# Two transformer blocks on one core: the relative-bias table made by one 12-row matmul and a replicating store

## What is computed

```python
h = rms_norm(x, norm1_g)
proj = h @ w_in                                    # [256, 3072]: q_d, k_d, v_d, q_m, k_m, v_m, 512 columns each
q = rms_norm(q, q_g); k = rms_norm(k, k_g)         # over each head's 64 columns, for both kinds of attention
dist = qpos[:, None] - kpos[None, :]               # 256 x 256
bias = bias_table[t5_bucket(dist)]                 # bias_table is [32, 12]: 32 buckets, 12 heads
logits = where(dist >= 0, q @ k.T * scale + bias, -1e30)
```

## Time and profile before

| | before |
|---|---|
| median of 3 runs | 1170.93 us (1169.04 to 1173.18) |
| span of the profiled execution (the page has no other time for it) | 1172.5 us |
| TensorE busy (matmuls) | 94% |
| VectorE, ScalarE, GpSimd busy | 49%, 35%, 4% |
| DMA | 239.54 MB, 204 GB/s over the span |

### The profile page before, as it was taken

How to read it: one execution, slowest core, us unless ns; L and a number is a source line. 1 busy time by engine, 2 the same in 40 slices (tenths; PEclk the granted TensorE clock), 3 DMA queues, 4 the chain that set the end, 5 groups by cost and what they waited for, 6 DMA issues and landing times.

```text
span 1172.5 us, 15803 instructions
## 1 busy us (share of the span) xinstructions
PE 1103.3 (94%) x6625; PEld 885.3 (76%) x6625; DVE 574.5 (49%) x724; ACT 415.6 (35%) x518; POOL 41.3 (4%) x55
## 2 busy tenths in 40 slices
PE   6998899999999999999999999977899999999996
PEld 5866688454444448999999998856688889999995
DVE  4546836222222226444444548478765655444443
ACT  3424513111111114434433444364344334433431
POOL 1202000000000000000000000010000000000000
PEclk8979798999999999999999999877899999999999
DMA  8548029879999985555555354431055544555540
GB/s 237 191 148 292 1 108 374 331 321 390 418 407 416 415 308 170 183 183 185 172 186 184 132 188 153 144 108 36 1 198 182 196 161 160 182 179 179 179 144 36
DMA packets 101489, 239.54 MB, mean 204 GB/s; under 512 B 10966, under 2 KB 56098, under 8 KB 86082
## 3 DMA queue, kind: packets, MB, share of 16 engines
q1 hardware_dynamic: 99170, 229.05, 54.5%
q0 software_dynamic: 2272, 9.83, 2.5%
HBM read 235.45 MB, written 3.41 MB: 204 GB/s over the span
## 4 chain that ended last, share of the span: by engine, by line
PE 82%; DVE 9%; ACT 3%; issue 2%; DMA 1%; POOL 1%; SPq 1%; POOLq 0%; ACTq 0%; DVEq 0%
PE banks L910 18%; PE banks L912 17%; PE banks L911 17%; PE banks L1114 10%; PE banks L1129 5%; PE banks L1104 3%; PE banks L1095 3%; PE banks L917 2%; PE banks L984 1%; DVE weights_lo L1463 1%; PE banks L995 1%; PE banks L1229 1%; DMA bias_rows<-stage 1%; POOL head_stats L501 1%; ACT weights_hi L608 1%
## 5 line engine op out<-in xcount | busy, mean ns | idle before, releaser
L1463 DVE TENSOR_TENSOR weights_lo<-raw_weights,weights_hi 128x2048 fp32r<-128x2048 f32 x116 | 265.5, 2291 | 264.8 <-ACT weights_hi L608 264.8
L608 ACT ACTIVATE weights_hi<-raw_weights 128x2048 fp32r<-128x2048 f32 x116 | 221.9, 1914 | 317.2 <-PE banks L912 311.6
L910 PE MATMUL banks<-weights_hi,normed_T_hi 128*128 128x256 f32 (+1 forms) x976 | 307.6, 315 | 1.1 <-DVE normed_T_lo L1480 0.6
L912 PE MATMUL banks<-weights_hi,normed_T_lo 128*128 128x256 f32 (+1 forms) x976 | 304.8, 312 | 0.0
L911 PE MATMUL banks<-weights_lo,normed_T_hi 128*128 128x256 f32 (+1 forms) x976 | 304.8, 312 | 0.0
L910 PEld LDWEIGHTS banks<-weights_hi,normed_T_hi 128*128 128x128 f32 x976 | 187.3, 192 | 13.8 <-issue 2.0
L911 PEld LDWEIGHTS banks<-weights_lo,normed_T_hi 128*128 128x128 f32 x976 | 187.2, 192 | 10.9
L912 PEld LDWEIGHTS banks<-weights_hi,normed_T_lo 128*128 128x128 f32 x976 | 186.9, 191 | 10.4
L1114 PE MATMUL banks<-expert_weights,stage 128*64 128x512 f32 x256 | 113.2, 595 | 0.0
L910 PE MATMUL banks<-weights_hi,ffn_hidden_T_hi 128*128 128x512 f32 x176 | 68.9, 392 | 3.0 <-DVE ffn_hidden_T_lo L1775 3.0
L911 PE MATMUL banks<-weights_lo,ffn_hidden_T_hi 128*128 128x512 f32 x176 | 68.7, 390 | 0.0
(11 more groups left out here) (305 smaller groups left out, 1597.1 us busy)
## 6 DMA issues: line engine op xcount, KB each, us to landing
raw_weights<-in_w_in SPq DMA_DIRECT2D x38, 1024.0 KB, 5.1
raw_weights<-in_ffn_w_gate SPq DMA_DIRECT2D x22, 1024.0 KB, 5.6
raw_weights<-in_ffn_w_up SPq DMA_DIRECT2D x22, 1024.0 KB, 5.6
raw_weights<-in_ffn_w_down SPq DMA_DIRECT2D x22, 1024.0 KB, 4.7
expert_weights<-in_w_gate SPq DMA_DIRECT2D x16, 1024.0 KB, 7.1
expert_weights<-in_w_up SPq DMA_DIRECT2D x16, 1024.0 KB, 9.2
expert_weights<-in_w_down SPq DMA_DIRECT2D x16, 1024.0 KB, 9.5
stage<-in_w_down SPq DMA_DIRECT2D x9, 1024.0 KB, 11.2
```

The lines of the kernel that those rows point to most:

```text
L608: ins = eng.activation(w_hi[:, slot, :], raw, ACT.Copy)
L910: eng.matmul(dst, x[0], w[0], start=first_one, stop=False)
L912: return eng.matmul(dst, x[1], w[0], start=False, stop=last_one)
L1463: ins = eng.tensor_tensor(w_lo[:, slot, :], raw, w_hi[:, slot, :], ALU.subtract)
```

## The change

The 12 matmuls, the spread table and the 12 copies become one matmul with 12 output rows, one copy of 12 x 384, and a store whose source repeats each of the 12 rows 128 times, so that DRAM receives the same 2.36 MB as before. That matmul and the transpose of the small vectors move between the first and the second half product of group 0; VectorE's part of both moves behind `feed(0)`. The store and load on GpSimd stand, in its order, ahead of the roots of all four q and k groups instead of between the second and the third. In each q or k group, VectorE makes the sums of squares of both tiles before it splits the next piece, and scales afterwards; each tile has a scratch place of its own.

```diff
-        bias_stage = LP[:, 0:N_BIAS * DIST_COLS].rearrange("p (h m) -> p h m", h=N_BIAS)
-        relb = LP[0:BUCKETS + 1, BS:BS + N_BIAS * P].rearrange("p (h q) -> p h q", h=N_BIAS)
+        bias_stage = LP[0:N_BIAS, 0:DIST_COLS]
+        onehot = LP[0:BUCKETS + 1, DIST_COLS:2 * DIST_COLS]
...
@@ gpsimd
-            for _ in range(2 * TILES):
-                root(hs[:, 0, 1, 0:8])
-            eng.wait_ge(bias_copied, N_BIAS)
-            eng.dma_start(bias_rows.rearrange("h p m -> p h m"), bias_stage).then_inc(bias_stored, 16)
+            eng.wait_ge(bias_copied, 1)
+            eng.dma_start(bias_rows, bias_stage.unsqueeze(1).broadcast_to([N_BIAS, P, DIST_COLS])).then_inc(bias_stored, 16)
             eng.wait_ge(bias_stored, 16)
...
             eng.dma_start(bias, skewed).then_inc(bias_loaded, 16)
             eng.wait_ge(normed, TILES * (N1 + 1))
             load_gain("norm2_g")
-            for _ in range(2 * TILES):
-                root(hs[:, 0, 1, 0:8])
+            for _ in range(4):
+                for t in range(TILES):
+                    root(hs[:, t, 1, 0:8])
@@ tensor
-            eng.wait_ge(vec_loaded, 16 * N_VEC)
-            eng.transpose(PS[:, 3, 0:V_ROWS], vec_rows[:, :], ident[0:V_ROWS, 0:V_ROWS]).then_inc(vec_T, 1)
             stay_warm(14, 2)
+            def small_tables():
+                eng.wait_ge(vec_loaded, 16 * N_VEC)
+                eng.transpose(PS[:, 3, 0:V_ROWS], vec_rows[:, :], ident[0:V_ROWS, 0:V_ROWS]).then_inc(vec_T, 1)
+                eng.wait_ge(rel_loaded, 32)
+                eng.matmul(PS[0:N_BIAS, 2, 0:DIST_COLS], relx[:, :], onehot[:, :], start=True, stop=True).then_inc(bias_ps, 1)
...
                 if c == 1:
                     eng.wait_ge(vec_ready, 1)
+                    eng.wait_ge(bias_copied, 1)
...
-                    if kh == 0 and c == 3:
-                        eng.wait_ge(rel_wide, 1)
-                        for h in range(N_BIAS):
-                            if h >= 2:
-                                eng.wait_ge(bias_copied, h - 1)
-                            eng.matmul(PS[:, 6 + h % 2, 0:DIST_COLS], relb[:, h, :], onehot[:, :], start=True, stop=True
-                                       ).then_inc(bias_ps, 1)
+                    if kh == 0 and c == 0:
+                        small_tables()
...
-            eng.wait_ge(bias_copied, N_BIAS)
@@ vector
             t8_split(T_N1, hT)
+            feed(0)
             eng.wait_ge(vec_T, 1)
...
-            feed(0)
-            eng.wait_ge(rel_loaded, 32)
-            eng.tensor_copy(relb[:, :, :], wide(relx[:, :], P)).then_inc(rel_wide, 1)
+            eng.wait_ge(bias_ps, 1)
+            eng.tensor_copy(bias_stage, PS[0:N_BIAS, 2, 0:DIST_COLS]).then_inc(bias_copied, 1)
...
+            def head_squares_of(c):
+                if c in (2, 5):
+                    return
+                for t in range(TILES):
+                    n = n_qk[0] + t
+                    eng.wait_ge(proj_sq, n + 1)
+                    eng.tensor_reduce(hs[:, t, 0, 0:8], tok[:, t, HALF:].rearrange("p (h d) -> p h d", d=HEAD),
+                                      AX_X, ALU.add).then_inc(proj_sq_read, 1)
+                    eng.wait_ge(proj_sq_read, n + 1)
+                    roots[0] += 1
+                    eng.tensor_scalar(hs[:, t, 1, 0:8], hs[:, t, 0, 0:8], 1.0 / HEAD, EPS, ALU.mult, ALU.add).then_inc(root_in, 1)
...
@@ vector, take_projection
-                    eng.wait_ge(proj_sq, n + 1)
-                    eng.tensor_reduce(hs[:, 0, 0, 0:8], tok[:, t, HALF:].rearrange("p (h d) -> p h d", d=HEAD),
-                                      AX_X, ALU.add).then_inc(proj_sq_read, 1)
-                    eng.wait_ge(proj_sq_read, n + 1)
-                    rsqrt(hs[:, 0, 1, 0:8], hs[:, 0, 0, 0:8], HEAD)
+                    eng.wait_ge(root_out, roots[0] - 1 + t)
...
             for c in range(6):
+                if c:
+                    head_squares_of(c - 1)
                 feed(2 * c)
                 if c:
                     take_projection(c - 1)
-                if c == 3:
-                    for h in range(N_BIAS):
-                        eng.wait_ge(bias_ps, h + 1)
-                        eng.tensor_copy(bias_stage[:, h, :], PS[:, 6 + h % 2, 0:DIST_COLS]).then_inc(bias_copied, 1)
```

More of the change, by code:

```diff
@@ L169, in two_blocks @@
         bias = view(6144, N_BIAS, SEQ)
-        bias_stage = LP[:, 0:N_BIAS * DIST_COLS].rearrange("p (h m) -> p h m", h=N_BIAS)
-        BS = N_BIAS * DIST_COLS
-        relb = LP[0:BUCKETS + 1, BS:BS + N_BIAS * P].rearrange("p (h q) -> p h q", h=N_BIAS)
-        onehot = LP[0:BUCKETS + 1, BS + N_BIAS * P:BS + N_BIAS * P + DIST_COLS]
-        lam_rows = LP[:, BS + N_BIAS * P + DIST_COLS:BS + N_BIAS * P + DIST_COLS + 4 * HEAD].rearrange("p (n d) -> p n d", n=4)
+        bias_stage = LP[0:N_BIAS, 0:DIST_COLS]
+        onehot = LP[0:BUCKETS + 1, DIST_COLS:2 * DIST_COLS]
+        lam_rows = LP[:, 2 * DIST_COLS:2 * DIST_COLS + 4 * HEAD].rearrange("p (n d) -> p n d", n=4)
         xgT = LP[:, 0:KT * RING * SLOTS].rearrange("p (k s) -> p k s", k=KT)
@@ L240, in two_blocks @@
         consts, root_in, root_out = sem("consts"), sem("root_in"), sem("root_out")
-        vec_T, vec_ready, rel_wide = sem("vec_T"), sem("vec_ready"), sem("rel_wide")
+        vec_T, vec_ready = sem("vec_T"), sem("vec_ready")
         bias_ps, bias_copied = sem("bias_ps"), sem("bias_copied")
@@ L1537, in take_projection @@
                     eng.tensor_tensor(tok[:, t, 0:HALF].rearrange("p (h d) -> p h d", d=HEAD),
-                                      bank.rearrange("p (h d) -> p h d", d=HEAD), wide(hs[:, 0, 1, 0:8], HEAD),
+                                      bank.rearrange("p (h d) -> p h d", d=HEAD), wide(hs[:, t, 1, 0:8], HEAD),
                                       ALU.mult).then_inc(proj_used, 1)
```

## The result

The changed kernel takes 1179.15 us (median of 9 runs, 1177.35 to 1181.44) against 1173.23 us of the kernel before (9 runs, 1169.04 to 1177.16): ratio 1.0052, 95% interval 1.0039 to 1.0066. It is 0.5% slower. The forecast was no change at 1171 with a range of 1151 to 1181; the time lies in the range, and the case that came is the third one, the slow store, to which I had given 0.30. The profiled span is 1177.4 us against 1172.5.

A forecast was written before the change was run, and what follows sets the result against it. TensorE was taken as the bound, its idle stretches, bias matmuls and low clock the time to win. Gains of 23.0 us, less the store's delay and 1.5 for the clock, gave 0.1: 1171 us at the median, range 1151 to 1181.

The forecast's parts named there:

- the slow store: Rival at GpSimd's wait ahead of the roots: shows slower from T = 34.6; at T = 39, net -7.9; chance 0.30.
- T: Time of GpSimd's bias store from 12 partitions, taken as 31 us, the middle by ratio of 12.9 and 74.
- net gain = 31.1 - T: Whole change: gains of 23.0 us, less the store's delay T - 9.6, less 1.5 for the clock.
- Start: Idle products right after the token transposes: first half product at 17.2 instead of 24.22, gain 7.0 us.
- Small tables: One vector transpose and one bias matmul between the first and second half product: cost 1.2 us.
- Bias matmuls and clock: TensorE's 12 bias matmuls from 65.17 go, 13.65 us, and the low clock after them, 1.3 us.
- VectorE order: Sums ahead of the split cover the roots: gain 0.8 after group 0, 1.2 after group 3, at most 0.2 after group 4.
- the 23.0: Sum of gains in us before the store's delay: 7.0 - 1.2 + 13.65 + 1.3 + 0.8 + 1.2 + 0.2.
- After the landing: GpSimd's load, gain load and roots, then scaling: TensorE's transposes end 6.6 us after the store lands.
- Clock after the hole: TensorE restarts at half clock after standing idle for the store: loss 1.5 us, between 0 and 2.6.
- Weights beside the store: About 1.3 weight pieces pass on the DMA queues beside the store; costed at nothing, up to 4 us if wrong.
- the fast store: Rival: source width does not matter, only engines; T 15.9, net 15.2 us; most of the 0.32 for faster.

The follow-up runs named there:

- changed_weights_early: The changed kernel, with SP issuing weight pieces 3 to 5 ahead of the router's and the gates' small loads; 1177.05 us, ratio 1.0026 to the kernel before.
- rows12_apart: The changed kernel, but the matmul gives 96 rows and the store reads 12 of them, 8 partitions apart, each 128 times; 1164.12 us, single run.
- rows24: The changed kernel, but the store reads 24 neighbouring rows, each 64 times; 1164.45 us, single run.
- rows96: The changed kernel, but the matmul gives 96 rows and the store reads all, each 16 times; 1160.76 us, ratio 0.9887 to the kernel before.
- tables_first: The changed kernel with the early start undone: small vectors and bias matmul ahead of idle products and first half product; 1179.38 us, ratio 1.0054.
- matmul_only: The kernel before with one 96-row bias matmul after group 3's first half product, its 96-row store at the old place; 1166.76 us, ratio 0.9935.
- order_only: The kernel before with only VectorE's new order, both tiles' sums ahead of the split; 1171.21 us, ratio 0.9980.
- rows96_roots_first: The changed kernel with 96 source rows and the four roots of groups 0 and 1 ahead of GpSimd's wait; 1151.30 us, ratio 0.9812.
- best_again: The kernel of rows96_roots_first measured a second time, unchanged; 1154.52 us, ratio 0.9829.
- roots_first: The changed kernel, but GpSimd serves the four roots of groups 0 and 1 before waiting for the store; 1168.60 us, ratio 0.9965.

## Why the prediction was right, and where it was off

**What decided was named rightly:** GpSimd's wait for the store, ahead of the roots, with T, the store's time, as the unknown. The formula, net gain = 31.1 - T, can be read against five kernels that differ in the store, and changed_weights_early in the order of SP's loads (gain in us of first logits against 115.71):

| kernel | T | 31.1 - T | measured |
|---|---|---|---|
| changed | 35.5 | -4.4 | -4.6 |
| changed_weights_early | 33.2 | -2.1 | -2.6 |
| rows12_apart | 20.8 | 10.3 | 10.7 |
| rows24 | 20.7 | 10.4 | 9.8 |
| rows96 | 14.8 | 16.3 | 15.9 |

**The term that was mis-sized is T:** 31 was taken, 35.5 measured. This turned "no change" into 0.5% slower; the point from which slower shows had been put at 34.6. The landing at 61.17 is also just past what I had written down as a sign of being wrong, after 60. The middle by ratio between 12.9 and 74 was a guess with nothing but its ends to rest on; that it came within 4.5 us was luck. The upper end was a rate for each partition, and rows12_apart refutes it: the same 12 rows, set apart, took 20.8. What it lacked was the start: I put 3.7 us around the transfer, but for four us after the issue the engines were full of weights, and the transfer itself needs 2.36/0.075 = 31.5 us. The 28.9 us estimated from the Trainium skill (SBUF — State Buffer, Door 1: The DMA port swizzle) were 8% short of that. Of the 8 us between 1171 and 1179.15, 4.5 are T, and 2.3 are the kernel before, whose own median rose from 1170.93 to 1173.23 with more runs; the other 1.3 are open.

**Start:** first half product at 17.2 predicted, 17.55 measured; store's issue 25.1 against 25.64. Right. But the term "gain 7.0" was true only in the sum. By itself it is 2.7, and with the slow store nothing (tables_first). The prediction had said in passing that with a long T the start matters less, because the store's issue moves with it; in tables_first it moved the other way, and the prediction did not see that an earlier store overtakes weights.

**Small tables:** 1.2 predicted; first to second half product 17.55 to 24.14, 6.6 us, less 5.47: 1.1.

**Bias matmuls and clock:** 14.95 predicted (13.65 + 1.3). From the transposes of group 1 to those of group 3 the changed kernel takes 79.86 to 102.55, 22.69 us; the kernel before 58.73 to 96.52, 37.79: 15.1 gained. matmul_only gets less because of its own wait and the clock behind it.

**VectorE order:** 0.8 + 1.2 + 0.2 predicted; 2.1 measured (order_only). In the changed kernel, group 3 to group 4 takes 11.77 us instead of 12.99 (109.51 in the kernel before): 1.2. From there to the first logits it takes 5.94 instead of 6.20: 0.3. Group 0 shows its part only where no store stands in front of it: in rows96_roots_first, group 0 to group 1 takes 11.77 instead of 12.61 us, 0.8. So every term of the 23.0 came within 0.4 us of its size. As a whole the sum was met in one profile of that version (23.3) and missed in the other (18.0, best_again), where a weight piece came late.

**After the landing:** the transposes were to end 6.6 us later, and ended 7.2 later (67.28 + 1.12). **Clock after the hole:** 1.5 predicted; the next two half products take 11.81 - 10.94 = 0.9 longer, and the transposes double from 0.60 to 1.11 each. In all, from the landing to the next transposes (79.86), 18.7 us where the prediction's terms give 19.0.

**Weights beside the store:** costed at nothing, and nothing in the changed kernel, since the longer wait covers it. Yet piece 5 came at 59.7 (its split on ScalarE starts there, released by its transfer), where the prediction had only the rest of piece 3 and piece 4 pass beside the store. The "up to 4 us" if that failed was far too low: with the wait gone, the slow store in roots_first is 17.0 us behind the fast one in rows96_roots_first (109.40 against 92.37). A reader who had taken the wait away on the strength of that "nothing" would have met this.

**The rivals:** the fast store is what rows96 does (15.9 was its T; 14.8 measured), reached by other means: its condition, that the source's width does not matter, is refuted. The slow store is the rival whose mechanism the runs bear out. Its case was a store at three sixteenths of the old rate because neighbouring partitions can give no more; measured are 75 of 355 GB/s, 3.4 sixteenths, and neighbours are what costs (rows12_apart, rows24), though in groups of four, not eight. Its price, -7.9 at T = 39, was too high by the 3.5 us in T.

## What to carry to other kernels

A DMA that reads few neighbouring partitions can be slow (here 35.5 us for 12 of them, 14.8 for 96), and it delays what shares the engines with it. Copies made by the matmul itself cost next to nothing (96 output rows took 0.84 us, 12 took 0.81) and spread the read. Look at a queue that waits for a DMA not by its engine's busy share but by who stands behind the wait, and put the wait behind them. And don't expect parts measured one at a time to add up where each alone runs into a wait that the others remove: here 11.7 us apart were 18 to 23 together.

## What was not expected of the hardware

GpSimd's power of 128 x 8 (one root) takes 1.65 us alone. The second of two in a row took twice that in this changed kernel, while VectorE worked at a weight split. GpSimd's two, and VectorE's split between them:

```profile
93.53 1.64 POOL L498 TENSOR_TENSOR head_stats<-head_stats,minus_half 128x8 f32<-128x8 f32 x1 [18.82 <-DVE head_stats L1528]
95.24 3.33 POOL L498 TENSOR_TENSOR head_stats<-head_stats,minus_half 128x8 f32<-128x8 f32 x1
```
```profile
94.79 2.29 DVE L1458 TENSOR_TENSOR weights_lo<-raw_weights,weights_hi 128x2048 fp32r<-128x2048 f32 x1 [0.61 <-ACT weights_hi L604]
```

The root that was under way when the split began was not slowed, and the split took its usual 2.29. The root that began inside the split ended 1.5 us after the split's end (97.08), about one root's time later. So the loss looks like a wait for the end of the split, and not like a root at a lower pace; the "2.1 to 2.5" of my expectation was a mean of the two. order_only has the same pair (1.64 and 3.33). In the kernel before, VectorE stood waiting during each root of the projection, and none took more than 1.66. With the two tiles' sums made first, the roots run beside the split. That the split is the cause was not tried by itself.
